# The S5 recurrence of a two-block transformer on one core: rotations of both parts in one operation, skip weights in TensorE's kernels, and a new order on two engines

## What is computed

```python
def _s5_mixer(h, w_in, lam_re, lam_im, log_dt, b_re, b_im, c_re, c_im, d, w_glu, b_glu):
    u = (h @ w_in)                                   # 512 x 1024
    lam_bar = jnp.exp(lam_dt)                        # lam, B, C are complex; 64 groups of 16 channels, 64 states
    def block_step(carry, u_blk):
        bu = jnp.einsum('btgh,gph->btgp', u_blk, b_bar)
        _, hs = lax.associative_scan(_s5_combine, (a_elems, bu), axis=1)
        hs = hs + a_pow[None] * carry[:, None]
        y = jnp.einsum('btgp,ghp->btgh', hs, c_mat).real
        return hs[:, -1], y
    ...
    y = ys + d * u                                   # the skip weights d
    g = jax.nn.gelu(y)
    val, gate = jnp.split(g @ w_glu + b_glu, 2, axis=-1)
    return val * jax.nn.sigmoid(gate)
```

## Time and profile before

| | us |
|---|---|
| median of 3 runs | 2395.39 |
| lowest and highest of them | 2386.42, 2395.86 |
| the profiled execution's own time | 2396.34 |
| span of its instructions | 2394.5 |
| PE busy in the span | 2298.5 (96%) |
| DVE busy in the span | 1488.8 (62%) |
| mean granted TensorE clock | 0.981 of full |

### The profile page before, as it was taken

The page is one execution under the profiler, slowest core; times in us unless marked ns, Lnnn a source line. Parts: engine busy times, 40 slices in busy tenths (PEclk is TensorE's granted clock), DMA queues, the critical chain, the costliest instruction groups (busy, mean ns, idle before and its releaser), DMA issues. The chain is left out here.

```text
span 2394.5 us, 34617 instructions
## 1 busy us (share of the span) xinstructions
PE 2298.5 (96%) x12714; PEld 1938.5 (81%) x12714; DVE 1488.8 (62%) x2209; ACT 1094.9 (46%) x1770; POOL 355.2 (15%) x374
## 2 busy tenths in 40 slices
PE   8999999999899999979899999999999999999998
PEld 7788888867788788877688888888877788888887
DVE  5786788698588768869636333437668853533443
ACT  5553554556555334643244323325558853421331
POOL 0120122111412212220010000010124521000001
PEclk9999999899999999989999999999999999999999
DMA  5345443232345555544122222222221212222221
GB/s 210 124 181 195 177 181 126 71 115 71 132 156 178 166 175 182 181 158 166 44 88 90 104 89 104 88 79 104 95 72 38 73 71 89 97 97 98 95 89 69
DMA packets 56346, 282.48 MB, mean 118 GB/s; under 512 B 7996, under 2 KB 19008, under 8 KB 28336
## 3 DMA queue, kind: packets, MB, share of 16 engines
q1 hardware_dynamic: 34144, 213.85, 24.8%
q0 software_dynamic: 12560, 58.80, 7.1%
q10 hardware_dynamic: 9536, 8.39, 1.1%
HBM read 265.15 MB, written 15.86 MB: 117 GB/s over the span
## 5 line engine op out<-in xcount | busy, mean ns | idle before, releaser
L517 PE MATMUL ps<-h_hi,w_hi 128*128 128x512 f32 (+1 forms) x2032 | 746.6, 367 | 22.7 <-DVE w_lo L2058 10.4
L2058 DVE TENSOR_TENSOR w_lo<-raw,w_hi 128x1024 fp32r<-128x1024 f32 x386 | 505.4, 1349 | 401.9 <-ACT w_hi L1237 401.7
L518 PE MATMUL ps<-h_lo,w_hi 128*128 128x512 f32 (+1 forms) x2032 | 735.3, 362 | 0.0
L519 PE MATMUL ps<-h_hi,w_lo 128*128 128x512 f32 (+1 forms) x2032 | 734.8, 362 | 0.0
L1237 ACT ACTIVATE w_hi<-raw 128x1024 fp32r<-128x1024 f32 x386 | 387.8, 1052 | 416.7 <-PE ps L519 415.3
L517 PEld LDWEIGHTS ps<-h_hi,w_hi 128*128 128x128 f32 x2032 | 389.0, 191 | 91.4 <-issue 21.0
L518 PEld LDWEIGHTS ps<-h_lo,w_hi 128*128 128x128 f32 x2032 | 389.5, 192 | 57.8 <-issue 0.7
L519 PEld LDWEIGHTS ps<-h_hi,w_lo 128*128 128x128 f32 x2032 | 389.3, 192 | 57.0
L517 PE MATMUL ps<-a_hi,w_hi 128*128 128x512 f32 (+1 forms) x1148 | 417.2, 363 | 4.3 <-DVE a_lo L2560 3.2
L518 PE MATMUL ps<-a_lo,w_hi 128*128 128x512 f32 (+1 forms) x1148 | 415.3, 362 | 0.0
L519 PE MATMUL ps<-a_hi,w_lo 128*128 128x512 f32 (+1 forms) x1148 | 415.3, 362 | 0.0
(11 more groups left out here) (413 smaller groups left out, 2545.5 us busy)
## 6 DMA issues: line engine op xcount, KB each, us to landing
raw<-weights_dram SPq DMA_DIRECT2D x161, 1024.0 KB, 4.8
ada_w<-ada_dram POOLq DMA_DIRECT2D x48, 1024.0 KB, 5.1
raw<-weights_dram SPq DMA_DIRECT2D x32, 704.0 KB, 3.9
par<-par_dram SPq DMA_DIRECT2D x8, 1152.0 KB, 6.7
par_dram<-plane POOLq DMA_DIRECT2D x10, 512.0 KB, 3.8
tab<-tab_dram SPq DMA_DIRECT2D x8, 512.0 KB, 5.7
x_tok<-x_rows_dram SPq DMA_DIRECT2D x4, 512.0 KB, 6.5
x<-x_in_dram SPq DMA_DIRECT2D x1, 2048.0 KB, 14.2
```

The lines of the kernel that those rows point to most:

```text
L517: nc.tensor.matmul(dst, w_hi[:, o:o + P], rhs_hi, start=start, stop=False)
L518: nc.tensor.matmul(dst, w_hi[:, o:o + P], rhs_lo, start=False, stop=False)
L519: return nc.tensor.matmul(dst, w_lo[:, o:o + P], rhs_hi, start=False, stop=last)
L2058: nc.vector.tensor_tensor(w_lo[:, o], raw[:, o], w_hi[:, o].bitcast(f32), SUB).then_inc(w_split, 1)
```

## The change

- **Both parts in one operation.** A block's real and imaginary parts now lie side by side in one tile of 1024 columns. `turn_in` and `turn_out` make the four products of 512 as two of 1024 (cosine by both, sine by both, the table row being read twice). The sums stay two of 512, now functions of their own (`join_in`, `join_out`). The free table is now signalled by `turned_out`, at the end of turn_out's products.
- **Skip weights on PE.** `skip5` is gone. POOL builds a tile `skip` of diagonal 32 by 32 blocks once, ahead of the stage, with four multiplications over 32 partitions by 256. `kernels5` has four more matmuls of 32 by 32 that add them in PSUM.
- **The order on PE.** inputs5(1) moves into `in_pair`, 12 products ahead of its end, and feature5(4) from round 0 to the place right behind `in_pair`.
- **The order on DVE.** Scan j + 1 runs ahead of the sums of block j, and the turns of the next blocks lie between products and their sums. The weight splits come behind join_out of rounds 1 and 3 and, the last, behind the low parts 0 to 3, which with all other `lo5` follow the last rotation.

The diff, cut to its core:

```diff
@@ SP
         if j >= 3:
-            sp.wait_ge(sem("t_re"), j - 2)
-            sp.wait_ge(sem("t_im"), j - 2)
+            sp.wait_ge(sem("turned_out"), j - 2)
@@ PE
             if j >= 3:
                 pe.wait_ge(sem("y5_read"), j - 2)
+            if j == 0:
+                pe.wait_ge(sem("skip_set"), 1)
...
+            for i in range(4):
+                rows = slice(32 * i, 32 * i + 32)
+                last = nc.tensor.matmul(bank(2 + (j + 1) % 2, 32, 32 * i, 32 * i + 32), skip[rows, 32 * j:32 * j + 32], ident[rows, rows],
+                                        start=False, stop=True)
             last.then_inc(sem("k_psum"), 1)
...
-            pe.wait_ge(sem("k_ready"), j + 1)
...
-        in_pair(("s5_in", "s5_in"), (2, 2), h_hi, h_lo, H_AT["s5_in"], {**SECOND, (1, 1, 2): lambda: inputs5(0)}, banks=((0, 1), (2, 3)))
+        in_pair(("s5_in", "s5_in"), (2, 2), h_hi, h_lo, H_AT["s5_in"], {**SECOND, (1, 1, 2): lambda: inputs5(0), (1, 1, 6): lambda: inputs5(1)}, banks=((0, 1), (2, 3)))
+        feature5(4)
         pe.wait_ge(sem("u_ready"), 4)
         kernels5(0)
-        inputs5(1)
         kernels5(1)
         for j in range(DC):
             if j + 2 < DC:
                 inputs5(j + 2)
-            if j + 4 < DC:
+            if 5 <= j + 4 < DC:
                 feature5(j + 4)
@@ DVE
+        def on_both(t):
+
+            return t.rearrange("p (h i c) -> p h i c", h=1, i=4).broadcast_to([P, 2, 4, P])
+
+        def turn_in(j):
...
+            nc.vector.tensor_tensor(blocks4(v), on_both(cos), both, MUL)
+            nc.vector.tensor_tensor(blocks4(tv), on_both(sin), both, MUL).then_inc(sem("rot_in"), 1)
+
+        def join_in(j):
...
+            nc.vector.tensor_tensor(v[:, 0:T], v[:, 0:T], tv[:, T:2 * T], ADD).then_inc(sem("v_ready"), 1)
+            nc.vector.tensor_tensor(v[:, T:2 * T], v[:, T:2 * T], tv[:, 0:T], SUB).then_inc(sem("v_ready"), 1)
...
+            nc.vector.tensor_tensor(blocks4(t), on_both(cos), blocks4(v), MUL)
+            nc.vector.tensor_tensor(blocks4(tg), on_both(sin), blocks4(v), MUL).then_inc(sem("turned_out"), 1)
...
-        rotate_in(0)
-        next_tile()
+        turn_in(0)
+        split_lo((0,))
+        join_in(0)
+        split_lo((1,))
+        g.after()
+        turn_in(1)
+        scan(0)
+        join_in(1)
+        turn_out(0)
         for j in range(DC):
             if j + 1 < DC:
-                rotate_in(j + 1)
-            skip5(j)
-            scan(j)
-            rotate_out(j)
-            if j in (1, 3, 5):
+                scan(j + 1)
+            join_out(j)
+            if j in (1, 3):
                 next_tile()
-            if j == 6:
-                lo5(0)
-                lo5(1)
-                lo5(2)
-        for j in range(3, DC):
+            if j + 2 < DC:
+                turn_in(j + 2)
+            if j + 1 < DC:
+                turn_out(j + 1)
+            if j + 2 < DC:
+                join_in(j + 2)
+        for j in range(4):
+            lo5(j)
+        next_tile()
+        for j in range(4, DC):
             lo5(j)
@@ POOL
+        for i in range(4):
+            rows = slice(32 * i, 32 * i + 32)
+            unit = ident[rows, rows].rearrange("p (j b) -> p j b", j=1).broadcast_to([32, DC, 32])
+            weight = vs("s5_d", 0, DC)[rows].rearrange("p (j b) -> p j b", b=1).broadcast_to([32, DC, 32])
+            ins = gp.tensor_tensor(as3(skip[rows, :], DC), unit, weight, MUL)
+        ins.then_inc(sem("skip_set"), 1)
```

More of the change, by code:

```diff
@@ L246, in build @@
     tab5 = [place(f"tab5{k}", D, offset=A0 + (36 + 4 * k) * KB) for k in range(3)]
[L247 to L250, removed]
+    v5 = [place(f"v5_{k}", 2 * T, offset=A0 + (48 + 4 * k) * KB) for k in range(3)]
+    t5 = [place("t5", 2 * T, offset=A0 + 60 * KB), sq]
+    skip = place("skip5", 32 * DC, offset=W0 + 4 * KB)
     k5 = [gl[:, 0:T], gl[:, T:2 * T]]
@@ L1006, in kernels5 @@
                     last = nc.tensor.matmul(as3(bank(2 + (j + 1) % 2, P, 32 * i, 32 * i + 32), Q5), b[:, o:o + 32], c4,
-                                            start=(part == 0), stop=(part == 1))
+                                            start=(part == 0), stop=False)
+            for i in range(4):
+                rows = slice(32 * i, 32 * i + 32)
+                last = nc.tensor.matmul(bank(2 + (j + 1) % 2, 32, 32 * i, 32 * i + 32), skip[rows, 32 * j:32 * j + 32], ident[rows, rows],
+                                        start=False, stop=True)
             last.then_inc(sem("k_psum"), 1)
@@ L1024, in outputs5 @@
                         last = nc.tensor.matmul(bank(yb, P - 1, 32 * i, 32 * i + 32, off=r * P + 1), b[:, o:o + 32],
-                                                t5[j % 2][part][:, i * P:(i + 1) * P - 1], start=False, stop=(r == Q5 - 1 and part == 1))
+                                                t5[j % 2][:, part * T + i * P:part * T + (i + 1) * P - 1], start=False, stop=(r == Q5 - 1 and part == 1))
             last.then_inc(sem("y5_done"), 1)
-        in_pair(("s5_in", "s5_in"), (2, 2), h_hi, h_lo, H_AT["s5_in"], {**SECOND, (1, 1, 2): lambda: inputs5(0)}, banks=((0, 1), (2, 3)))
+        in_pair(("s5_in", "s5_in"), (2, 2), h_hi, h_lo, H_AT["s5_in"], {**SECOND, (1, 1, 2): lambda: inputs5(0), (1, 1, 6): lambda: inputs5(1)}, banks=((0, 1), (2, 3)))
+        feature5(4)
         pe.wait_ge(sem("u_ready"), 4)
         kernels5(0)
-        inputs5(1)
         kernels5(1)
@@ L2749, in _, with blocks4 @@
         table = lambda j: tab5[j % 3]
-        def rotate_in(j):
+        def blocks4(t):
+            return t[:, :].rearrange("p (h i c) -> p h i c", h=2, i=4)
+        def on_both(t):
+            return t.rearrange("p (h i c) -> p h i c", h=1, i=4).broadcast_to([P, 2, 4, P])
+        def turn_in(j):
             v, cos, sin = v5[j % 3], table(j)[:, 0:T], table(j)[:, T:2 * T]
-            re, im = (ps[:, 4 * T:8 * T].rearrange("p (i c) -> p i c", i=4)[:, :, part * P:(part + 1) * P] for part in range(2))
+            both = ps[:, 4 * T:8 * T].rearrange("p (i b) -> p i b", i=4)[:, :, 0:2 * P].rearrange("p i (h c) -> p h i c", h=2)
             dve.wait_ge(sem(f"tab_landed{j % 3}"), 16 * (j // 3 + 1))
@@ L2780, in scan, with turn_out @@
             for part in range(2):
-                v = v5[j % 3][part][:, :]
+                v = v5[j % 3][:, part * T:(part + 1) * T]
                 dve.wait_ge(sem("v_ready"), 2 * j + part + 1)
                 nc.vector.tensor_tensor_scan(v, decay5[j % 2][:, :], v, 0.0, MUL, ADD).then_inc(sem("scanned"), 1)
-        def rotate_out(j):
-            re, im = t5[j % 2]
-            cos, sin, v = table(j)[:, 0:T], table(j)[:, T:2 * T], v5[j % 3]
+        def turn_out(j):
+            t, v, cos, sin = t5[j % 2], v5[j % 3], table(j)[:, 0:T], table(j)[:, T:2 * T]
             if j:
@@ L3245, in _ @@
         ins.then_inc(sem("pool_set"), 1)
+        gp.wait_ge(sem("pool_set"), POOL_SET["s5"])
+        for i in range(4):
[4 more added lines that the diff above has]
+        ins.then_inc(sem("skip_set"), 1)
         gp.wait_ge(sem("scanned"), 2 * DC)
```

28 lines of the change are left out of this document (7 added, 21 removed).

## The result

| | before | changed |
|---|---|---|
| median | 2395.01 us (8 runs, 2386.42 to 2399.11) | 2380.56 us (8 runs, 2376.38 to 2381.94) |
| the profiled execution's own time | 2396.34 | 2380.91 |
| span | 2394.5 | 2379.2 |

The ratio is 0.9939, with a 95% interval from 0.9928 to 0.9950: 14.5 us less, 0.61%. Forecast were 11.65 us less, 2383.7 us, in a range from 2377 to 2391. Later the changed kernel was measured twice more beside fresh runs of the kernel before: 0.9941 (0.9925 to 0.9957) and 0.9960 (0.9947 to 0.9973), the second time 9.0 us between medians (2391.72 and 2382.71). So the size is less certain than one interval says, and 12 us, a ratio of 0.995, fits all three.

What follows compares the result with a forecast made beforehand. PE was taken to bound rounds 0 to 3 and DVE the end, with PE gaps at the start. 13.3 - 1.0 - 0.35 - 0.3 = 11.65 us off 2396.34 leaves 2384.7, median 2383.7, range 2377 to 2391.

Steps and rivals of the forecast that it cites:

- The bound: Over the stage: PE gaps at the start, PE bounds rounds 0 to 3, DVE sets the last 34.67 us.
- Prices on DVE: Wide product 1.135 us for two at 1.20, two scans 2.25; a block falls from 9.93 to 9.19 us.
- Start: Stage start up to inputs5(3): PE's gaps go, inputs5(3) at 1089.4 for 1096.64, 7.2 us gained.
- Middle: Three PE rounds with features 5 to 7, each 0.15 us longer; the gain falls to 6.8 us.
- End: Rounds 5 to 7: DVE idles 2.3 us before scan 5, then 25.3 us; stage ends at 1154.5, 13.3 us gained.
- term (3): Small DVE waits behind the decay row, 0.1 us a block, 0.3 us taken off the gain.
- term 1: Lower PE clock on outputs5(7) behind a 2.8 us gap: 0 to 2.6 us off, taken as 1.0.
- term 2: POOL's four multiplications slow DVE operations under the norm ahead of in_pair: 0 to 1.0 us off, taken as 0.35.
- (b): Rival on DVE: wide products no faster than two, or slower; gain 5 to 6 us, time 2389.5; chance 0.15.
- (d): Rival behind the stage: gated layer waits for low parts or a weight tile; 0 to 2 us, inside the forecast's range.
- (a): Rival: clock holds to the end, wide products at 1.07, decay row sooner; gain 14 to 17 us, time 2380; chance 0.11.
- (c): Rival at PE's start: clock falls at 1072, 12 us more a round, two rounds make 2408; chance 0.04.

Runs made afterwards that it cites:

- x5: The changed kernel with low parts 0 to 2 back in round 6 and the last weight split back in round 5; median 2383.15 us.
- x1: The changed kernel with each wide DVE product of 1024 made as two of 512 in the same place; median 2382.13 us.
- x6: The changed kernel with decay row j + 2 at the head of ACT's round j, ahead of the feature block's copy; median 2381.84 us.
- x7: As x6, and with inputs5(6) moved ahead of outputs5(3) on PE; medians 2377.03 and 2376.68 us.
- x4: The changed kernel with skip weights back on DVE behind the next block's scan, without skip matmuls and POOL's products; median 2383.63 us.
- x2: The changed kernel with PE's start taken back to the old order; median 2388.12 us.

## Why the prediction was right, point by point

- **The bound** was right. PE's gaps were the place of the gain: none of its waits lies in rounds 1 to 3, before or after, and at the end DVE's work went onto the stage (x5).
- **Prices on DVE** held: 1.135 for a wide product, 2.25 for two scans, 9.19 for a block (9.18 from one turn_in at 1093.69 to the next at 1102.87). Of the 0.74 us saved a block, 0.26 is the fusing and 0.47 the skip and the waits, so these are nearer to two thirds than to the half that the prediction gave them. PSUM as a source made no difference at 1024 elements either. The Trainium skill, "VectorE: DVE Perf Modes", section on the TRN2 errata, gives a fixed cost of 58 cycles from SBUF and 120 from PSUM. The 0.065 us found here from both sources fits the 58 cycles (as an estimate 0.060 us at that page's 0.96 GHz), and not the 120.
- **Start:** priced 7.2 us up to inputs5(3). Counted from D, which takes out the shift ahead of the stage, inputs5(3) starts at 20.31 us (1085.42 - 1065.11) for 27.09: 6.8.
- **Middle:** a round with a feature block is 12.36 us (1093.00 to 1105.36) for the 12.32 priced. The skip matmuls are 0.19 and not 0.15. Inputs5(6) starts 57.36 us after D (1122.47) for 63.59 before: 6.2 us gained, of 6.8 reckoned.
- **End:** the wait for the decay row was foreseen and sized at 2.3 us; it was 2.77, because feature block 7, and with it ACT's row, came 0.5 us later than reckoned, which is most of the 0.6 us missing above. From there to the last sum 25.3 us were reckoned, 25.6 measured. The 0.3 between them is term (3) in size but not in place: it stands in the last block alone (1144.09 to 1144.86 is 0.77 us for 0.60, 1146.00 to 1147.26 is 1.26 for 1.135).
- **What comes off** is the step that failed, by its size. The clock (term 1, "I take 1.0") cost nothing: the slow row is there, 4.11 us for the first half of outputs5(6), but PE was waiting for DVE's sums until 1144.92 anyway, and outputs5(7) ran at full clock. The place was wrong too: it stood for outputs5(7). That the clock cost nothing is in part luck of the place. In x1 and x6 the first half of outputs5(6) came behind the same wait for ACT's copies (1.77 and 1.78 us), but at full clock; it ended sooner, so the wait behind it was 2.67 and 2.40 us long instead of 0.72; and the low clock then fell on the two halves on the path, for 1.6 us, inside the prediction's 0 to 2.6. In all three profiles of the changed kernel it falls on the first half, where PE has time to spare. What puts it here or there was not tried. POOL's products (term 2, "I take 0.35") ran from 1052.69 to 1055.60, the last 2.1 us of them beside DVE's norm, whose operations kept their 0.39 us between starts: nothing again. By the Trainium skill, "SBUF — State Buffer", section "SBUF: two separate sides", a VectorE operation with two SBUF inputs and a GpSimd one that reads SBUF exclude each other. That would have given the upper end, 1.0 us; nothing of it shows in this place. Without both terms, and with the decay row's extra 0.5 us, the sum comes to 13.3 - 0.3 - 0.5 = 12.5, and the stage gave 12.27.
- **The other 2.2 us** of the 14.5 belong to no step. Profiles of unchanged parts differ by more than that, and the third comparison gave 9.0.
- **Rivals.** (b) did not occur, and (d) is worth 0.2 us at most (72.23 for 72.08 behind G). (a) gave the time of the first comparison, 2380, but the stage's gain is 12.27 and not 14 to 17. Of its three reasons only the clock came true, and only in that it cost nothing on the path: wide products were no cheaper and the decay row came no sooner. (c) did not occur at the start; x1 and x6 show that the clock can take 1.6 us at the other end. The chance of 0.56 for "within 0.5%" was a reading of 11.65 against 12; the stage's 12.27 lies on the other side of that line by less than any of the comparisons can tell.

## What to carry to other kernels

Where two engines hand work to and fro, price a change as two lists with their meeting points, not as a sum of parts: PE's start was worth 1.4 us alone and 5.8 with the rest. An operation of 0.27 us that stands on one engine between two steps of another makes the other wait for all that it stands behind, here a scan (1.20 to 3.08 us a block, of which 0.9 reached the end). When the last wait before the end is shortened on one engine, look at what the clock of the next one does behind the gap that this opens. And cut profiles at fixed events of the program: the stretch repeats to 0.01 us here where the events themselves stand up to 3 us apart in two profiles of one kernel.

## What was not expected of the hardware

- **The clock behind a wait of 2.4 to 2.7 us.** At the end of the stage the granted clock went low for the halves behind it in x1 and x6 (1.94 to 2.89 and 2.96 us; 2.42 to 3.11 and 3.03), and not behind waits of 0.47 to 0.72 us at the same place in the changed kernel and x7. The length of a wait alone does not decide: behind 1.77 us the first half of outputs5(6) was slow in the changed kernel (4.11 us, granted clock 0.58) and fast in x5 and x1, behind 1.78 fast in x6 and x7, and in x4 a first half behind 2.71 us took 3.67 and the next, behind 3.08 us, 2.42.
- **The clock at the stage's start differs between executions of one kernel.** Two stretches behind S in x7's first profile (columns as above):

```profile
1058.37:1060.37 2.00, 2.00 (x10) 2.00 (x11) 2.00 (x6) 1.18 (x4) 0.43 (x1) 0.58 1.00 416
1060.37:1062.37 2.00, 2.00 (x13) 2.00 (x12) 2.00 (x6) 1.44 (x4) 0.00 (x0) 0.56 1.04 431
```

and in its second:

```profile
1055.22:1057.22 2.00, 2.00 (x15) 1.98 (x16) 2.00 (x6) 1.18 (x4) 0.42 (x1) 1.00 0.97 402
1057.22:1059.22 2.00, 2.00 (x18) 1.96 (x16) 2.00 (x6) 1.45 (x4) 0.00 (x0) 1.00 1.08 449
```

0.58 and 0.56 against 1.00, with the same work ahead. D comes 1.17 us later after S in the first (11.09 for 9.92), as in x2 and x4 and in no other profile. Why the same gap has one outcome or the other was not tried.
- **Matmuls of 32 by 32** add 0.19 us for a set of four, a third of the 0.57 us of the eight matmuls of four times the columns ahead of them (1077.04 to 1077.61).
